# Seven quarter products instead of eight for most input slabs of the second mixer, with the weight sums on GpSimd

## The chip, the cores and the metric

One core of a Trainium2 chip runs the whole program in one launch. The metric is the device time of that launch in microseconds (us). TensorE multiplies matrices (stationary weights are loaded, then columns of the moving operand stream past them) into PSUM, which has eight banks of 128 partitions x 512 fp32. VectorE (DVE), ScalarE (ACT) and GpSimd (POOL) do the rest, and SyncE's queue (SP) issues nearly all loads from HBM. Engines wait for each other by semaphores only. All data are fp32.

## The reference

256 tokens of width 1024 pass through two blocks. The first is a gated feed-forward, a mixer (RWKV-7 time mixing beside dilated attention) and another feed-forward. The second block has two layers, each a mixer and then a dense feed-forward (layer 0) or eight experts of which two are chosen per token (layer 1). The part of the layer's mixer that the change concerns:

```python
def _mixer(h, pos, rel_table, w_in, b_gate, ...):
    z = h @ w_in                      # 1024 x 5792
    dq, dk, dv, cq, ckv, kr, gl = jnp.split(z, IN_SPLIT_IDX, axis=-1)
    ...
    o_a = _diff_attention(dq..., dk..., dv..., ...)     # 8 heads, two score maps each
    o_b = _mla(cq, ckv, kr, ...)                        # 8 heads
    g = jax.nn.sigmoid(gl + b_gate)
    g_a, g_b = g[..., :D_MODEL], g[..., D_MODEL:]
    m = g_a * (o_a @ w_branch_diff) + g_b * (o_b @ w_branch_mla)
    return m @ w_out
```

`dq` and `dk` have 1024 columns each, `gl` 2048. In the first block's time mixing the state recurrence (`wkv7_scan`) is computed in chunks of 64 tokens, with small 64 x 64 products per head.

## The kernel before, in words

**Layout.** `h_cm` holds the 256 tokens' activations, channels in the partitions: 8 tiles of 128 channels x 256 tokens. Weights come in slabs of 1024 x 512 (2 MB, 128 partitions x 4096) into a ring of four slots. A list, `stream`, fixes their order; SP goes through it and before load n waits for the last reader of load n - 4 (`last_reader`, L3168 to L3171). For a layer of the second block the order is lat, latr, dqk 0, dv 0, dqk 1, dv 1, dqk 2, uq, dqk 3, ukv, gate slabs g2 0 to 3, bmla, bdiff 0 and 1, out2 0 and 1. Slab dqk a holds the queries and keys of heads 2a and 2a + 1; the four gate slabs hold the 2048 gate columns.

**A plain slab** (`product_cm`, L312) is four output tiles of 128 columns, two to a bank, each the sum of eight matmuls of 128 x 128 weights by 128 x 256 activations. The compiler splits every fp32 matmul into two instructions, so a slab is 64 instructions in the profile. ScalarE copies the dqk banks to SBUF (L2188) and takes the gates' sigmoid straight from PSUM (L2200).

**Strassen's scheme in the feed-forwards.** Three feed-forwards already use one level of it (`pe_up_seven`, L468): the product of a slab, cut into 2 x 2 quarters, with the activations, cut into 2 x 2 quarters, is made of seven quarter products instead of eight. A unit is 7 x 8 matmuls of 128 x 128 by 128 x 128, 112 instructions. VectorE makes four sums of weight quarters (L556 to L561), and eight additions that put the seven products together (L571 to L585).

**Order of the mixer** (`pe_mixer2`, from L1978): it is written out by hand, one program per engine. On TensorE: lat, latr, dqk 0, scores 0, dv 0, dqk 1, turn 0 (transposes of the softmax weights, L2036), scores 1 (L2026), output 0 (L2047), dv 1, dqk 2, turn 1, scores 2, output 1, uq, dqk 3, turn 2, scores 3, output 2, ukv, g2 0, turn 3, MLA scores 0 (L2063), output 3, g2 1, MLA turn 0 (L2073), MLA scores 1, MLA output 0 (L2085), g2 2, the sums for the norm of the differential heads' output (L2140), MLA turn 1, the first half of g2 3, MLA output 1, the second half of g2 3, bmla, then, behind a wait for `oa_ready`, bdiff 0 and 1, and out2. Banks go round in rotation (`next_bank`), and each filling waits until the previous content of its bank was read.

**The normed output OA.** After MLA output 1 ScalarE copies it (L2215), loads a table and takes a square root (L2263); VectorE takes the reciprocal (L2394), multiplies (L2396) and scales (L2397), which sets `oa_ready`. Then `dve_merge` (L1658, L1663, L1667) multiplies the branch products by the gates.

**MLA weights.** VectorE masks the scores (L2355), takes row maxima (L2269), ScalarE the exponentials (L2172), VectorE the reciprocal of the sums and two multiplications (L2364), and TensorE turns the result (L2073).

**The recurrence** (`pe_rwkv_chunks`): eight groups of four heads by two chunks in a software pipeline. Per group and pair half, the key products (L1258) are 16 matmuls of 64 columns; the steps of the triangular solve are rounds of eight (L1237); the solved step is two such rounds with the same weights; the queries (L1317) are 16 matmuls of 64 columns.

**GpSimd** does no arithmetic on the data: it issues some loads (norm rows, L1968; the per-layer embedding tile, L1974) and clears a row.

## Time and profile before

| | us |
|---|---|
| median of 3 runs (2611.89 to 2613.22) | 2612.46 |
| the profiled execution's own time | 2612.26 |
| its span | 2610.2 |
| TensorE busy, share of the span | 97% |
| VectorE busy | 37% |
| ScalarE busy | 14% |
| GpSimd busy | 2% |

The span is divided roughly so: first feed-forward to 205 us, first mixer to 690, second feed-forward to 905, mixer of layer 0 from 908 to 1191, dense feed-forward to 1425, mixer of layer 1 from 1433 to 1717, experts to the end. A row of the profile's lists names the engine, the line of the kernel, the instruction, what it writes and reads and how often it occurs; "idle before" tells how long the engine stood still just before, and what ended that.

### The profile page before, as it was taken

The numbers are of one execution on the slowest core, as the hardware profiler recorded it, in microseconds if no ns is written. First come the engines' busy times: TensorE is split into PE (matmuls) and PEld (weight loads), VectorE is DVE, ScalarE is ACT, GpSimd is POOL, SyncE is SP. The second block draws the span as 40 slices with busy tenths as digits, with TensorE's granted clock in tenths as the row PEclk, the third lists the DMA queues.
The fourth block names the chain that finished last, engine by engine and source line by source line (L and its number), as shares of the span: only waits on it lengthen the run. The fifth ranks groups of instructions, "written<-read, shape, count | busy, mean of one in ns | idle before, by whom it ended". The sixth has DMA issues, their size and how long they took to land.

```text
span 2610.2 us, 74146 instructions
## 1 busy us (share of the span) xinstructions
PE 2539.9 (97%) x33934; PEld 2154.1 (83%) x33934; DVE 964.1 (37%) x1792; ACT 365.7 (14%) x842; POOL 42.4 (2%) x74
## 2 busy tenths in 40 slices
PE   8999999999999999999999999999999999999998
PEld 8966778887698477875994778759999998999997
DVE  5663464633477723244676233440000001000002
ACT  1001241210100023311000234120000001000000
POOL 0000000000100000000000000010000000000000
PEclk9999999999999999999999999999999999999999
DMA  6445242014344543325435434379999999999995
GB/s 259 148 144 196 105 152 103 4 36 153 142 174 153 189 169 128 133 113 193 179 108 187 165 142 166 145 246 373 427 427 426 425 426 397 427 427 427 426 425 251
DMA packets 58053, 607.72 MB, mean 233 GB/s; under 512 B 7364, under 2 KB 7492, under 8 KB 12352
## 3 DMA queue, kind: packets, MB, share of 16 engines
q1 hardware_dynamic: 52272, 587.74, 56.4%
q0 software_dynamic: 5648, 18.04, 2.2%
q8 instruction: 105, 1.72, 0.3%
q14 instruction: 28, 0.23, 0.0%
HBM read 599.66 MB, written 6.09 MB: 232 GB/s over the span
## 4 chain that ended last, share of the span: by engine, by line
PE 92%; DMA 4%; DVE 2%; issue 1%; ACT 1%; POOL 0%; SPq 0%; DVEq 0%; ACTq 0%; POOLq 0%
PE bank L312 22%; PE bank L2681 18%; PE bank L468 16%; PE bank L2694 9%; PE bank L495 7%; PE bank L322 5%; DMA slot<-in_experts 3%; PE bank L1648 3%; PE bank L1237 3%; PE bank L1634 1%; PE bank L965 1%; PE bank L1258 1%; PE bank L2613 1%; PE bank L1317 0%; PE bank L2026 0%
## 5 line engine op out<-in xcount | busy, mean ns | idle before, releaser
L2681 PE MATMUL bank<-arena,slot 128*64 128x84 f32 x14336 | 545.5, 237 | 13.7 <-issue 8.1
L2681 PEld LDWEIGHTS bank<-arena,slot 128*64 128x64 f32 x14336 | 531.8, 137 | 21.1 <-issue 16.9
L312 PE MATMUL bank<-h_cm,slot 128*128 128x256 f32 x1984 | 436.4, 381 | 0.3 <-ACT h_cm L359 0.2
L312 PEld LDWEIGHTS bank<-h_cm,slot 128*128 128x128 f32 x1984 | 376.5, 191 | 58.4 <-issue 7.9
L2880 DVE TENSOR_TENSOR ff<-ff,bank 128x168 f32<-128x168 f32 x112 | 36.9, 330 | 639.4 <-PE bank L2681 635.3
L2694 PE MATMUL bank<-ff,arena 128*64 128x84 f32 x5376 | 218.1, 237 | 2.6 <-issue 2.6
L2694 PEld LDWEIGHTS bank<-ff,arena 128*64 128x64 f32 x5376 | 205.7, 137 | 9.0 <-issue 4.4
L468 PE MATMUL bank<-arena 128*128 128x128 f32 x1584 | 187.7, 275 | 0.0
L468 PEld LDWEIGHTS bank<-arena 128*128 128x128 f32 x1584 | 182.2, 192 | 0.0
L468 PEld LDWEIGHTS bank<-h_cm,slot 128*128 128x128 f32 x1056 | 125.5, 198 | 9.9 <-issue 9.9
L468 PE MATMUL bank<-h_cm,slot 128*128 128x128 f32 x1056 | 129.4, 283 | 3.5 <-DVE h_cm L371 2.8
L312 PE MATMUL bank<-arena,slot 128*128 128x256 f32 x608 | 132.7, 379 | 0.0
L312 PEld LDWEIGHTS bank<-arena,slot 128*128 128x128 f32 x608 | 115.0, 190 | 17.0 <-issue 1.6
L2817 ACT ACTIVATE ff<-bank 128x168 f32<-128x168 f32 x112 | 34.8, 311 | 668.6 <-PE bank L2681 668.6
L322 PE MATMUL bank<-slot,h_cm 128*128 128x512 f32 (+1 forms) x288 | 119.3, 571 | 0.7 <-ACT h_cm L355 0.6
L322 PEld LDWEIGHTS bank<-slot,h_cm 128*128 128x128 f32 x288 | 53.9, 190 | 60.8 <-issue 60.0
L495 PE MATMUL bank<-arena,ff 128*128 128x512 f32 x180 | 86.5, 592 | 0.0
L1648 PE MATMUL bank<-slot,arena 128*128 128x512 f32 x192 | 82.9, 592 | 0.0
L539 ACT ACTIVATE ff<-arena 128x512 f32<-128x512 f32 x33 | 20.8, 631 | 403.3 <-DVE arena L585 403.3
L1648 PEld LDWEIGHTS bank<-slot,arena 128*128 128x128 f32 x192 | 36.3, 190 | 44.5 <-issue 44.0
L2694 PE MATMUL bank<-ff,x_tm 128*64 128x84 f32 x1792 | 69.9, 236 | 0.6 <-issue 0.6
L495 PEld LDWEIGHTS bank<-arena,ff 128*128 128x128 f32 x180 | 34.2, 190 | 43.1 <-issue 37.6
(452 smaller groups left out, 2581.0 us busy)
## 6 DMA issues: line engine op xcount, KB each, us to landing
slot<-in_experts SPq DMA_DIRECT2D x112, 2048.0 KB, 16.9
arena<-in_experts SPq DMA_DIRECT2D x84, 1024.0 KB, 12.7
slot<-in_ffn SPq DMA_DIRECT2D x22, 2048.0 KB, 8.2
x_tm<-in_experts SPq DMA_DIRECT2D x28, 1024.0 KB, 12.5
slot<-in_ffn SPq DMA_DIRECT2D x22, 1024.0 KB, 4.8
slot<-in_dense SPq DMA_DIRECT2D x11, 2048.0 KB, 7.7
slot<-in_dqk SPq DMA_DIRECT2D x8, 2048.0 KB, 8.0
slot<-in_g SPq DMA_DIRECT2D x8, 2048.0 KB, 7.7
```

The source lines that it names most:

```text
L312: ins = pe.matmul(ps[0:m, j * S:(j + 1) * S], w[:, k * width + c0:k * width + c0 + m], rhs[:, k, :], start=k == 0, stop=k == ks - 1)
L322: ins = pe.matmul(ps[:, 0:n], lhs[:, k, t * P:(t + 1) * P], w[:, k * width + c0:k * width + c0 + n], start=start and k == 0, stop=stop and ...
L468: ins = pe.matmul(ps[:, g, :], left[q][:, k, g, :], right[q][:, k, :], start=k == 0, stop=k == 3)
L495: ins = pe.matmul(PS[DOWN_BANK[q]][:, :], left[q], right[q], start=first, stop=u == U_DENSE - 1, skip_group_check=True)
L965: ins = pe.matmul(ps[:, j * S:(j + 1) * S], w[:, c0:c0 + P], h_cm[:, k, :], start=k == 0, stop=k == KD - 1)
L1237: ins = pe.matmul(ps[rows, h * width + c0:h * width + c0 + 64], left(rows, a, p, i), right(rows, a, p, i), start=True, stop=True)
L1258: ins = pe.matmul(ps[chunk_rows(c), (2 * x + i) * 64:(2 * x + i + 1) * 64], left[rows, k, tok], right[rows, k, tok], start=True, stop=True)
L1648: ins = pe.matmul(ps[:, :], src[:, k, t * P:(t + 1) * P], w[:, k * 512:(k + 1) * 512], start=k == 0, stop=k == KD - 1)
L2681: ins = pe.matmul(bank[64 * c:64 * c + 64, m * PLACES:(m + 1) * PLACES], weights[:, c0:c0 + 64], CURRENT[:, k, :], start=k == 0, stop=k == ...
L2694: ins = pe.matmul(PS[4 + d // 4][64 * c:64 * c + 64, (d % 4) * PLACES:(d % 4 + 1) * PLACES], weights[:, c0:c0 + 64], ff[:, 2 + par, kk * P ...
L2817: act.activation(ff[:, par, 0:2 * PLACES], PS[par][:, 0:2 * PLACES], ACT.Silu).then_inc(silu_ready, 1)
L2880: v.tensor_tensor(ff[:, 2 + par, 0:2 * PLACES], ff[:, par, 0:2 * PLACES], PS[2 + par][:, 0:2 * PLACES], ALU.mult).then_inc(hidden_ready, 1)
```

## The change

It has four parts.

- Slabs dqk 1, 2 and 3 and all four gate slabs of both layers go by Strassen's scheme: 112 instructions instead of 64 per slab, and four banks instead of two. Slab dqk 0 and the others stay as they are. Gate slab 3 is cut at the fourth product (1, 2, 6, 7 before MLA output 1, then 4, 5, 3).
- The four sums of weight quarters of such a slab are made by GpSimd, into a slot of the same ring: the list of loads gets an entry without a source behind each of the seven slabs, SP passes over it, and GpSimd waits for the weights and for the last reader four entries before. It also makes the four sums of activations, once per layer, in the space of the norm rows; these rows are therefore loaded only once gate slab 3 was read.
- VectorE puts the products together (eight operations of 128 x 256 per slab) at places written into its program. ScalarE no longer copies dqk 1 to 3, and takes the gates' sigmoid from SBUF, once all four banks of a slab are done. The merge waits for the sigmoids (`gates_ready`).
- In the recurrence, pairs of matmuls that have the same weights become one of twice the columns, whose moving operand lies in two places: key products, solved step, queries. The buffer XV moves for this.

```diff
+                if (name, n) in SEVEN_SLABS:
+                    stream.append(((f"sum_{name}{l}", n), None, 0))
...
-                for x, (left, right) in enumerate(((KK, DEC), (K, DEC), (KK, R), (K, R))):
+                for m, left in enumerate((KK, K)):
                     for i in range(2):
                         for c in range(2):
                             tok, k = chunk_tokens(t, c), k0 + 2 * a + i
-                            ins = pe.matmul(ps[chunk_rows(c), (2 * x + i) * 64:(2 * x + i + 1) * 64],
-                                            left[rows, k, tok], right[rows, k, tok], start=True, stop=True)
+                            at = k * S + tok.start
+                            ins = pe.matmul(out[chunk_rows(c), :, m, i, :], left[rows, k, tok],
+                                            two_places(rows, 2048 + at, 8 * 2048 + at), start=True, stop=True)
...
-                by_chunk(ps, a, P, 0, lambda rows, a, p, i: TT[a][rows, p, i, :], head_of(A_TM, g))
-                filled(by_chunk(ps, a, P, HD, lambda rows, a, p, i: TT[a][rows, p, i, :],
-                                lambda rows, a, p, i: XV[a][rows, p, i, :]), ("WU", j, a))
+                for h, (p, i) in enumerate(HEADS):
+                    for c in range(2):
+                        rows, head = chunk_rows(c), (k0 + 2 * a + i) * P + 64 * p
+                        ins = pe.matmul(ps[rows, h * P:(h + 1) * P], TT[a][rows, p, i, :],
+                                        two_places(rows, 2 * 2048 + t * D + head, XV_AT[a] + h * CHUNK), start=True, stop=True)
...
+        def pool_slab_sums(pool, l):
+            add, sums = pool.tensor_tensor, named("x_quarters")
...
+            for name, n in SEVEN_SLABS:
+                weights = first_load[f"{name}{l}", n]
+                load, w = slab_sums(l, name, n)
+                s, done, before = weights % SLOTS, slot_loaded[load % SLOTS], 16 * (load // SLOTS)
+                pool.wait_ge(slot_loaded[s], 16 * (weights // SLOTS + 1))
+                pool.wait_ge(*last_reader[load - SLOTS])
+                add(w[0], quarter_w(s, 1, 0), quarter_w(s, 1, 1), ALU.add).then_inc(done, 4)
+                pool.wait_ge(done, before + 4)
+                add(w[1], w[0], quarter_w(s, 0, 0), ALU.subtract).then_inc(done, 4)
+                pool.wait_ge(done, before + 8)
+                add(w[3], quarter_w(s, 0, 1), w[1], ALU.subtract).then_inc(done, 4)
+                pool.wait_ge(done, before + 12)
+                add(w[2], quarter_w(s, 0, 0), quarter_w(s, 1, 0), ALU.subtract).then_inc(done, 4)
...
+        def pe_slab_seven(pe, l, name, n, products):
...
+            for q in products:
+                b, c = slab_product(q)
+                key = (name, l, n, b)
+                ps = fill(pe, key, next_bank()) if c.start == 0 else PS[job[key][0]]
+                if (name, n) == SEVEN_SLABS[0] and q == 6:
+                    pe.wait_ge(named("x_quarters"), 4 * l + 4)
+                if q in (6, 7):
+                    pe.wait_ge(slot_loaded[load % SLOTS], 16 * (load // SLOTS) + (8 if q == 6 else 16))
+                out = ps[:, c].rearrange("p (g s) -> p g s", g=2)
+                for g in range(2):
+                    for k in range(4):
+                        ins = pe.matmul(out[:, g, :], left[q][:, k, g, :], right[q][:, k, :], start=k == 0, stop=k == 3)
...
+            if b == 0:
+                ch.step(v.tensor_copy(G_PART[:, 3], product(1)))
+                ins = v.tensor_tensor(out(0, 0), G_PART[:, 3], product(2), ALU.add)
+            elif b == 1:
+                ch.step(v.tensor_tensor(G_PART[:, 0], G_PART[:, 3], product(6), ALU.add))
+                ins = v.tensor_tensor(G_PART[:, 1], G_PART[:, 0], product(7), ALU.add)
+            elif b == 2:
+                drained(dve, (name, l, n, 1))
+                v.tensor_tensor(out(1, 0), G_PART[:, 1], product(4), ALU.subtract)
+                v.tensor_tensor(out(1, 1), G_PART[:, 1], product(5), ALU.add)
+                ins = v.tensor_tensor(G_PART[:, 2], G_PART[:, 0], product(5), ALU.add)
+            else:
+                drained(dve, (name, l, n, 2))
+                ins = v.tensor_tensor(out(0, 1), G_PART[:, 2], product(3), ALU.add)
+            free(ins, (name, l, n, b))
...
             mla_turn(1)
-            g2_bank(3, 0)
+            pe_slab_seven(pe, l, "g2_", 3, SEVEN[0:4])
             mla_out(1)
-            g2_bank(3, 1)
+            pe_slab_seven(pe, l, "g2_", 3, SEVEN[4:7])
...
             def g2(s):
-                for tile in range(4 * s, 4 * s + 4, 2):
-                    ps = full(act, ("g2", l, tile))
-                    for j in range(2):
-                        ins = act.activation(gates2[:, tile + j, :], ps[:, j * S:(j + 1) * S], ACT.Sigmoid,
-                                             bias=col(f"b_gate{l}", tile + j))
-                    free(ins, ("g2", l, tile))
+                for b in range(4):
+                    drained(act, ("g2_", l, s, b))
+                for tile in range(4 * s, 4 * s + 4):
+                    ins = act.activation(gates2[:, tile, :], gates2[:, tile, :], ACT.Sigmoid, bias=col(f"b_gate{l}", tile))
+                ins.then_inc(named("gates_ready"), 1)
...
             diff_weights(3)
+            gate(0, 0, 1, 2, 3)
             diff_turned(3)
-            mla_weights(0)
+            mla_weights(0, lambda: gate(1, 0, 1))
+            gate(1, 2, 3)
             mla_turned(0)
-            mla_weights(1)
+            mla_weights(1, lambda: gate(2, 0, 1))
+            gate(2, 2, 3)
...
             mla_turned(1)
-            dve.wait_ge(named("oa_rms"), l + 1)
+            gate(3, 0, 1)
+            dve.wait_ge(named("oa_stages"), 4 * l + 3)
...
-            for tile in range(0, 16, 2):
-                drained(dve, ("g2", l, tile))
+            gate(3, 2, 3)
+            dve.wait_ge(named("gates_ready"), 4 * (l + 1))
```

In `mla_weights` the two additions of the slab (`meanwhile`) stand between the row maxima and the wait for the exponentials; `SEVEN` is the order of the products, 1, 2, 6, 7, 4, 5, 3, two to a bank.

## Rows read from the trace of the kernel before

**Rows 1.** The page: busy time, granted clock, chain by engine, a gate slab's load.

```profile
PE 2539.9 (97%) x33934; PEld 2154.1 (83%) x33934; DVE 964.1 (37%) x1792; ACT 365.7 (14%) x842; POOL 42.4 (2%) x74
PEclk9999999999999999999999999999999999999999
PE 92%; DMA 4%; DVE 2%; issue 1%; ACT 1%; POOL 0%; SPq 0%; DVEq 0%; ACTq 0%; POOLq 0%
slot<-in_g SPq DMA_DIRECT2D x8, 2048.0 KB, 7.7
```

**Rows 2.** Stretches: layer 0's mixer and a plain slab (TensorE alone), a recurrence period (all engines).

```profile
908.00:1158.10 250.10, 249.38 (x1175) 1.00 0.38 143
960.57:974.38 13.81, 13.81 (x65) 1.00 0.24 97
...
475.30:488.70 13.40, 12.32 (x432) 11.53 (x432) 8.37 (x24) 3.49 (x11) 0.00 (x0) 1.00 0.02 6
```

**Rows 3.** The chain that ended last: start, us, what.

```profile
14.12 139.95 PE bank L468 x1232
...
1109.30 48.54 PE bank L312 x224
...
1223.40 137.81 PE bank L468 x1232
```

**Rows 4.** Timeline around the OA chain of layer 0.

```profile
1109.22 7.17 PE L312 MATMUL bank<-h_cm,slot 128*128 128x256 f32 x32
1113.18 12.95 DVE L2394 RECIPROCAL arena<-arena 128x2048 f32<-128x2048 f32 x1 [11.91 <-ACT arena L2263]
1126.17 2.29 DVE L2396 TENSOR_TENSOR arena<-arena 128x2048 f32<-128x2048 f32 x1
1128.50 1.29 DVE L2397 TENSOR_SCALAR arena<-arena,cols 128x2048 f32<-128x2048 f32 x1
1129.70 2.48 DVE L1658 TENSOR_TENSOR arena<-bank,arena 128x512 f32<-128x512 f32 x4
```

**Rows 5.** Groups of instructions: VectorE's sums in the second feed-forward; GpSimd's MEMSET.

```profile
L556 DVE TENSOR_TENSOR arena<-slot 128x1024 f32<-128x1024 f32 x7 | 8.5, 1219 | 0.0
L573 DVE TENSOR_TENSOR arena<-arena,bank 128x256 f32<-128x256 f32 x6 | 2.5, 420 | 0.2
...
L2960 POOL MEMSET arena<- 1x1024 f32 x1 | 0.9, 942 | 0.0
```

**Rows 6.** Timeline: dqk slab 3 with the turn behind it, gate slab 0.

```profile
1033.72 0.82 PE L2036 MATMUL bank<-consts,arena 128*128 128x128 f32 x6
1033.92 0.59 ACT L2188 COPY arena<-bank 128x512 f32<-128x512 f32 x1 [6.32 <-PE bank L312]
...
1044.42 13.98 PE L312 MATMUL bank<-h_cm,slot 128*128 128x256 f32 x64
```

**Rows 7.** Timeline around mla_weights 0 and gate slab 1.

```profile
1068.80 1.83 DVE L2364 TENSOR_TENSOR arena<-arena,ff 128x512 f32<-128x512 f32 x2
...
1076.63 1.47 PE L2073 MATMUL bank<-consts,arena 128*128 128x128 f32 x12
...
1076.84 0.84 ACT L2200 ACTIVATE arena<-bank,cols 128x256 f32<-128x256 f32 x2 [4.35 <-PE bank L312]
...
1080.66 0.65 PE L2085 MATMUL bank<-arena 128*64 128x256 f32 x4
```

**Rows 8.** Timeline of one recurrence period: rounds, queries, key products.

```profile
463.46 0.54 PEld L1237 LDWEIGHTS bank<-ff,xn 64*64 64x64 f32 x16
463.92 0.55 PEld L1237 LDWEIGHTS bank<-xn,ff 64*64 64x64 f32 x16
...
466.23 0.69 PE L1317 MATMUL bank<-arena,ff 64*64 64x64 f32 x32 [0.22 <-ACT ff L1440]
466.69 0.55 PEld L1237 LDWEIGHTS bank<-ff,xn 64*64 64x64 f32 x16
...
468.50 1.06 PEld L1258 LDWEIGHTS bank<-arena 64*64 64x64 f32 x32
...
```

More of the change, by code:

```diff
@@ L232, in two_blocks @@
         stream = []
+        SEVEN_SLABS = [("dqk_", 1), ("dqk_", 2), ("dqk_", 3)] + [("g2_", n) for n in range(4)]
         def slabs(name):
@@ L763, in two_blocks, with two_places @@
         ff_flat = ff[:, :, :].rearrange("p n s -> p (n s)")
-        X1, XV = ([ff_flat[:, (2 * a + i) * 256:(2 * a + i + 1) * 256].rearrange("p (h i s) -> p h i s", h=2, i=2)
-                   for a in range(2)] for i in range(2))
+        X1 = [ff_flat[:, 512 * a:512 * a + 256].rearrange("p (h i s) -> p h i s", h=2, i=2) for a in range(2)]
+        XV_AT = (24576, 26368)
+        XV = [arena[:, at:at + 256].rearrange("p (h i s) -> p h i s", h=2, i=2) for at in XV_AT]
+        def two_places(rows, first, second):
+            return bass.AP(arena, rows.start * 13 * 2048 + first, [[13 * 2048, CHUNK], [second - first, 2], [1, CHUNK]])
         WU = [ff_flat[:, 1024 + a * 512:1024 + (a + 1) * 512].rearrange("p (h i d) -> p h i d", h=2, i=2) for a in range(2)]
@@ L1323, in queries @@
                 drained(pe, ("WU", *g))
-                by_quadrant("QG", g, ((0, decayed, key_block(0), True, True), (1, decayed, head_of(B_TM, g), True, True)))
+                j, a = g
+                t, k0 = PAIRS[j]
+                ps = [fill(pe, ("QG", *g, c), next_bank()) for c in range(2)]
+                last = {}
+                for i in range(2):
+                    for p, c in QUADRANTS:
+                        head = (k0 + 2 * a + i) * P + 64 * p
+                        out = ps[c][64 * p:64 * p + 64, 0:256].rearrange("p (u i s) -> p u i s", u=2, i=2)
+                        last[c] = pe.matmul(out[:, :, i, :], decayed(chunk_rows(c), a, p, i),
+                                            two_places(chunk_rows(c), 4 * 2048 + t * D + head, key_block_at(a, p, i)),
+                                            start=True, stop=True)
+                for c in range(2):
+                    filled(last[c], ("QG", *g, c))
             def outputs(g):
@@ new lines, in slab_product @@
+        def slab_product(q):
+            r = SEVEN.index(q)
+            return r // 2, slice((r % 2) * S, (r % 2 + 1) * S)
+        def pe_slab_seven(pe, l, name, n, products):
+            weights = first_load[f"{name}{l}", n]
+            load, w = slab_sums(l, name, n)
+            s = weights % SLOTS
+            pe.wait_ge(slot_loaded[s], 16 * (weights // SLOTS + 1))
+            left = {1: quarter_w(s, 0, 0), 2: quarter_w(s, 0, 1), 3: w[3], 4: quarter_w(s, 1, 1), 5: w[0], 6: w[1], 7: w[2]}
+            right = {1: quarter_x(0, 0), 2: quarter_x(1, 0), 3: quarter_x(1, 1), 4: X_SUM[:, 3], 5: X_SUM[:, 0],
+                     6: X_SUM[:, 1], 7: X_SUM[:, 2]}
+            for q in products:
[10 more added lines that the diff above has]
+                        ins = pe.matmul(out[:, g, :], left[q][:, k, g, :], right[q][:, k, :], start=k == 0, stop=k == 3)
+                if c.start or q == 3:
+                    filled(ins, key)
+            if products[-1] == 3:
+                released((f"{name}{l}", n), (name, l, n, 3))
+                released((f"sum_{name}{l}", n), (name, l, n, 3))
@@ L2235, in act_mixer2 @@
             dv(1)
-            dqk(2)
             diff_out(1)
```

93 lines of the change are left out of this document (66 added, 27 removed).

## The prediction

> **What bounds the kernel now.** I read the page first: TensorE is busy for 97% of the span and is 92% of the chain that ended last, at the granted clock's upper level, 2.4 GHz, in every slice [rows 1]. Next a stretch of the second block's mixer in layer 0: 249.38 of 250.10 us are TensorE's [rows 2], and layer 1 runs the same program. So time goes there only if matmul time goes or a wait comes in; VectorE is busy for 37% of the span, GpSimd for 2% [rows 1]. Last the recurrence (the WKV chunks): a period of 13.4 us with TensorE busy for 12.3 [rows 2], small waits between. The profiled execution took 2612.26 us around a span of 2610.2; the median of the runs is 2612.46, so I sum against 2612.3.
>
> **Plain slab against Strassen slab.** A dqk or gate slab is 64 instructions of 128x256 (the compiler splits each fp32 matmul in two) and takes 13.81 us [rows 2], one of four such stretches of layer 0 with the same length. Seven quarter products are 7 x 8 x 2 = 112 instructions of 128x128. The same form runs in the dense block: 1232 in 137.81 us for 11 units, 12.53 us per unit, and 139.95 us, 12.72, in the first feed-forward [rows 3]. I take 12.65: these slabs have waits like the first one's. Saved per slab 13.81 - 12.65 = 1.16 us, between 1.09 and 1.28. That is 8% of the slab and not the 12.5% of the count of products, because a 128-column instruction costs 112 to 114 ns where half of a 256-column one costs 108 (13.81 / 64 / 2). Six of the seven slabs in each of two layers: 12 x 1.16 = **-13.9 us** (-13.1 to -15.4).
>
> **The seventh slab (gate slab 3) gives nothing.** Its halves surround the last MLA output. From its second half (1109.22) a chain runs beside TensorE: ScalarE's copy, table load and Sqrt, VectorE's reciprocal of 12.95, multiply 2.29, scale 1.29, ended at 1128.50 + 1.29 = 1129.79 [rows 4]. TensorE covers it with 32 instructions of the slab and 64 of bmla, 96 x 48.54 / 224 = 20.8 us [rows 3], to 1130.1: 0.3 us of cover to spare. Now three products, 48 x 113 ns = 5.4, and bmla's 13.9 make 19.3 against the chain's 20.6: a wait of 1.3 us before bdiff appears. Ahead of the MLA output stand four products, 64 x 113 ns = 7.2 us, instead of 6.9. Together +0.3 for the first half, and the old spare 0.3 is all that is won behind it: **0**, up to +0.5 per layer. VectorE's adds for banks 0 and 1 are done before the reciprocal can start (Sqrt ends 4 us after the MLA output begins); those for 2 and 3 come behind the scale, 4 x 0.42 = 1.7 us, then ScalarE's four sigmoids, 1.7 us (two take 0.84 [rows 7]), then the merge of bmla, 2.48 us [rows 4, 5]. TensorE needs none of it until the first bdiff bank is merged, about 7 us on, so this costs nothing, with about 1 us of cover.
>
> **VectorE's adds, 0.** Eight operations of 128x256 with PSUM input at 0.415 to 0.42 us [rows 5], 3.4 us per slab, lie under the slab's own 12.65 us. The last one ends 0.4 us behind product 3; before, ScalarE's copy of 0.59 us stood there and the scores began right behind the turn of 0.82 us [rows 6]. ScalarE loses its dqk copies. Banks: a slab now takes four of the eight in rotation. I followed the fills; the tight one is the fourth MLA score bank, which waits for the gate bank that VectorE adds behind mla_weights.
>
> **Weight sums on GpSimd.** The trace has no arithmetic on GpSimd. Below, its MEMSET of 1024 elements, one stream: 0.94 us. Above, three streams (two read, one written), 2.83 us. VectorE takes 1.22 us for the same sum [rows 5]. I take the middle, 1.9 us an operation, 7.5 a slab. What hides it: the ring. A sum's slot is free when the load four places before is read, and TensorE needs two sums after two products (+3.6 us) and all four after three (+5.4). The tightest is gate 0: slot free with dqk 3 at 1033.72, slab read from 1044.42, all four by 1049.8, so 16.1 us for four, 4.0 us each [rows 6]; gate 2 and 3 wait for their weights (a load of 7.7 us [rows 1] after the slab two before), which leaves 5.1 us each, dqk 3 about 4.8. So up to 4.0 us per operation the sums cost 0. The Trainium skill, "GPSIMD Engine Reference", Elementwise side-by-side cycle accounting, puts a two-input fp32 add at 4497 ns for 2048 elements, about 2 times VectorE, and says to use VectorE for such work; no trace here shows it, and by it the sum is the same, since its estimate of 2.3 us for 1024 also lies under 4.0. The four sums of x, half as large, run 40 us before they are read.
>
> **The ring.** Every load waits for a reader four places before, now with the sums in the count: gate 1's weights wait for the sum of dqk 3 (landing about 1042, read from 1061), bmla's for gate 2. Each has over 10 us in hand at 7.7 us a load. The norm rows now load behind gate 3, with the ple tile queued behind them on GpSimd; about 40 us pass until TensorE turns it. 0.
>
> **Stalls.** ScalarE now has four sigmoids behind the last bank instead of two, then the copies on which the attention outputs wait: VectorE's last add ends 0.6 us after the slab, the sigmoids take 1.7, two copies like the one of 0.59 [rows 6] 1.2, together 3.5 us, where TensorE arrives 4.0 us after it [rows 7], and about 3.3 us after gate slab 0; if a table load comes behind the waits, it is late by up to a microsecond, twice per layer. And VectorE must get mla_weights 0 out before gate slab 1 ends, with two adds of the slab ahead of its multiplies (slack about 2 us, from 5 [rows 7]). I book 1.0 us per layer, between 0 and 3: **+2.0** (0 to +6).
>
> **The recurrence.** The diff also joins pairs of 64-column matmuls with the same weights. Key products: 32 instructions in 1.06 us, 33 ns each, two quadrants at work. Joined, 16 of 128 columns at 113 / 2 = 56 ns: 0.90 us. The solved step: 16 in 0.46 us, twice, 0.92, to 0.90; queries 32 in 0.46, to 16 x 28 = 0.45 [rows 8]. Of the two key products per group one lies in the stretch where TensorE waits for the levels of the solve (1.1 us of the period in all [rows 2]), so its saving goes into the wait. That leaves some 0.25 us for each of 8 groups: **-2.0** (+1 if two-place operands stream worse, -3.9 if all counts). XV's move changes no work.
>
> **Sum.** 2612.3 - 13.9 + 0 + 2.0 - 2.0 = **2598.4 us**. What follows is a chain in which everything moves up, the expert loads too: they start on slots that TensorE frees. 0.2% (5.2 us) is about what a measurement of this kernel can tell from no change.
>
> **Rivals.**
> A. *VectorE held up by GpSimd.* Gate slab 2's sums start about 8 us after gate slab 0 ends and last 7.5 to 9 us; in that stretch VectorE has mla_weights' two multiplies, both inputs in SBUF, 1.83 us [rows 7]. If each waits for a running sum of 1.9 us, mla_weights is 3.8 us late against 2 us of slack, in each layer, and some short stalls elsewhere: +4 to +6, 2603. For it: these are the only two-input SBUF operations near a wait. Against: other such work has 10 us of slack. The Trainium skill, "SBUF — State Buffer", section on the two separate sides, states that VectorE with two SBUF inputs and GpSimd take a shared port pair as an exclusive lock for a whole instruction; no row of before shows it, and it is this rival's mechanism. 20%.
> B. *The sums come late: slower.* Place: TensorE's wait for the sums before products 6 and 7. It costs nothing up to 4.0 us per operation, then 4 us for each us more at gate 0, and from 4.8 and 5.1 at three more slabs. At 5.2 it eats 7 us per layer, all that the change brings. At 5.6, twice my upper bound: (6.4 + 3.2 + 2 x 2.0) x 2 = 27, less 14: 2625. Against: four times VectorE's time. 4%.
> C. *VectorE in the turn's place.* If each slab's last add comes a microsecond late for the scores or sigmoids behind it, 1.16 is given back and only the recurrence stays: 2610. Against: VectorE idles 7 us and more ahead of most slab ends. 8%.
> D. *More than forecast.* Slabs at 12.53, no stalls, all of the recurrence: 2612.3 - 15.4 - 3.9 = 2593. 12%.
> The forecast itself, 2595.5 to 2601.5: 56%.
>
> **Numbers.** The range from 2592 to 2605 holds the forecast, D and nearly all of A. Faster: forecast, A, D = 88%; same 8% (C and the edge of A); slower 4% (B).
>
> **What would show it.** Right: 112 instructions per slab in 12.5 to 12.7 us; GpSimd sums between 0.94 and 2.83 us; a wait of 1.3 us before bdiff released by VectorE's scale; mixers of about 244 us; periods of 13.2. Wrong: a TensorE wait released by GpSimd; the two multiplies of mla_weights longer than 0.92 us each; a wait before the MLA turn; a slab that takes over 13 us.

## The result, and the profile after

The changed kernel takes **2625.2 us** (2624.4 to 2625.7, 5 runs) where the kernel before took 2612.5: the ratio is 1.0049, 95% interval 1.0037 to 1.0060. It is slower by 0.5%; the prediction was 2598.4, faster, with a range up to 2605.

The page of the changed kernel: busy time, granted clock, instruction queue (packets, MB), chain by engine, the largest group.

```profile
PE 2519.3 (96%) x34094; PEld 2156.9 (82%) x34094; DVE 1041.3 (40%) x1904; ACT 359.5 (14%) x830; POOL 185.6 (7%) x138
PEclk9999999999999999999999999999999999999999
q8 instruction: 134, 2.20, 0.3%
PE 89%; DVE 5%; issue 3%; ACT 2%; DMA 1%; POOL 0%; SPq 0%; DVEq 0%; ACTq 0%; POOLq 0%
L2818 PE MATMUL bank<-arena,slot 128*64 128x84 f32 x14336 | 547.9, 237 | 33.2 <-issue 31.2
```

The same two rows of the kernel before, which had no part in the prediction.

```profile
q8 instruction: 105, 1.72, 0.3%
L2681 PE MATMUL bank<-arena,slot 128*64 128x84 f32 x14336 | 545.5, 237 | 13.7 <-issue 8.1
```

Beside [rows 1], TensorE's busy time is 20.6 us less, so the arithmetic saving arrived; all of it lies ahead of the experts, in which TensorE is busy for 829.4 us before and 829.5 us after. "Issue" is 3% of the chain where it was 1%. (DVE is at 5% where it was 2%, but that is no loss of this size: in the mixers the chain now runs through VectorE while TensorE works beside it.) The last row names the place: the experts' up-projections (L2681 before, L2818 after), the same instructions, with 31.2 us of waiting for nothing that the profile shows, where it was 8.1. The change touches no line of the experts. And TensorE's program came in 134 packets of 16 KB instead of 105.

Where the time went can be seen from the starts of the same pieces in both chains (before, after, difference in us): first block's output projection 658.59, 653.26, **-5.3**; layer 0's mixer 908.95, 903.57, -5.4; its output projection 1158.28, 1149.78, -8.5; layer 1's 1683.42, 1672.84, **-10.6**; first expert matmul 1753.94, 1742.04, **-11.9**; end +13.6. From the first expert matmul to the end of the span the kernel before takes 856.3 us and the changed one 881.8: **25.5 us** are lost in code that the change does not touch. Of the 20.6 us only 11.9 arrive at the experts; the other 8.7 are new idle time of TensorE, nearly all in three waits of each of the two mixers (2.3, 0.8 and 1.2 us, further below).

The changed kernel's stretches that answer to [rows 2]: both mixers and one recurrence period (us, then TensorE busy, its weight loads, VectorE, ScalarE, GpSimd, granted clock).

```profile
903.57:1149.78 246.21, 241.69 (x1505) 205.66 (x1506) 122.59 (x199) 68.49 (x168) 73.18 (x35) 0.99 0.39 148
1423.60:1672.84 249.24, 244.72 (x1505) 207.67 (x1506) 128.11 (x201) 70.14 (x169) 73.64 (x36) 0.98 0.40 149
486.15:499.03 12.88, 11.99 (x368) 11.37 (x369) 8.49 (x24) 3.50 (x11) 0.00 (x0) 1.00 0.02 4
```

The two mixers run the same program. Some 2.5 us of the second one's 249.24 lie at its beginning, where its first 80 matmuls take 20.5 us at a granted clock of 0.52 (1423 to 1430); in the run with the loop's head at slot 0 (below), with the same code there, they take 18.0 us at 1.00. So these 2.5 us are not the slabs' doing.

The changed kernel's chain: three Strassen slabs (dqk 1, gate 1, gate 2), then the stretch around the second expert pair's beginning.

```profile
955.35 12.51 PE bank L1799 x112
...
1054.62 14.03 PE bank L1799 x112
...
1074.86 12.70 PE bank L1799 x112
...
1946.08 8.79 issue
1954.87 3.35 PE bank L2818 x44
1958.21 1.06 issue
1959.28 3.27 PE bank L2818 x84
1962.55 1.53 PE bank L2831 x42
1964.08 1.25 issue
```

TensorE stands still for 8.79 us with no releaser, where its loop over pairs of experts goes back to its head, and again for 8.60 us at 2384.13; smaller gaps follow. Three more rows of the changed kernel: a window behind that stand and one behind a wait in layer 0's mixer (us, TensorE busy, granted clock), and the instruction queue from 1945 to 2010.

```profile
1955.00:1958.00 3.00, 3.00 (x44) 0.50 0.98 407
...
1054.00:1056.00 2.00, 2.00 (x12) 0.56 0.03 8
...
q8 instruction: 9, 0.15, 1.0%
```

Behind the stand the granted clock is 0.50, the lower of its two levels. Nine packets of program arrive where the kernel before has none. Some ten microseconds after the stand the loads of data fall to 50 GB/s for a short while: they wait for slots that TensorE frees, and SyncE's queue waits for TensorE for up to 19.2 us there. These loads run at 427 GB/s otherwise, and the lost time is not made up.

### The profile page after: what moved, and what is told of

It reads as the page before. It is cut to its first block, busy times and chain, and to the rows that moved or that the text cites. A ratio compares the mean times of both kernels' runs of the same rounds, so it can differ in the third digit from the quotient of the medians.

```text
span 2623.8 us, 74738 instructions
## 1 busy us (share of the span) xinstructions
PE 2519.3 (96%) x34094; PEld 2156.9 (82%) x34094; DVE 1041.3 (40%) x1904; ACT 359.5 (14%) x830; POOL 185.6 (7%) x138
## 4 chain that ended last, share of the span: by engine, by line
PE 89%; DVE 5%; issue 3%; ACT 2%; DMA 1%; POOL 0%; SPq 0%; DVEq 0%; ACTq 0%; POOLq 0%
PE bank L2818 20%; PE bank L471 16%; PE bank L315 13%; PE bank L2831 10%; PE bank L498 7%; PE bank L1799 5%; PE bank L325 5%; PE bank L1677 3%; PE bank L1245 2%; PE bank L1663 1%; DVE arena L2531 1%; DMA slot<-in_experts 1%; PE bank L973 1%; PE bank L2750 1%; PE bank L1268 1%
## 5 line engine op out<-in xcount | busy, mean ns | idle before, releaser
L2818 PE MATMUL bank<-arena,slot 128*64 128x84 f32 x14336 | 547.9, 237 | 33.2 <-issue 31.2
L2818 PEld LDWEIGHTS bank<-arena,slot 128*64 128x64 f32 x14336 | 533.8, 138 | 40.1 <-issue 39.7
L315 PE MATMUL bank<-h_cm,slot 128*128 128x256 f32 x1088 | 243.0, 385 | 1.3 <-ACT h_cm L358 0.6
L315 PEld LDWEIGHTS bank<-h_cm,slot 128*128 128x128 f32 x1088 | 208.9, 193 | 35.1 <-issue 6.2
L2831 PE MATMUL bank<-ff,arena 128*64 128x84 f32 x5376 | 212.1, 237 | 6.0 <-issue 5.8
L2831 PEld LDWEIGHTS bank<-ff,arena 128*64 128x64 f32 x5376 | 200.9, 137 | 11.9 <-issue 10.0
L471 PEld LDWEIGHTS bank<-h_cm,slot 128*128 128x128 f32 x1056 | 123.4, 196 | 8.9 <-issue 8.9
L471 PE MATMUL bank<-h_cm,slot 128*128 128x128 f32 x1056 | 127.1, 280 | 2.8 <-DVE h_cm L374 2.8
L1799 PE MATMUL bank<-xn,slot 128*128 128x128 f32 x896 | 102.9, 275 | 0.0
L1799 PEld LDWEIGHTS bank<-xn,slot 128*128 128x128 f32 x896 | 101.3, 192 | 0.3 <-issue 0.3
L1799 PEld LDWEIGHTS bank<-h_cm,slot 128*128 128x128 f32 x672 | 80.4, 197 | 2.5 <-issue 2.3
L1799 PE MATMUL bank<-h_cm,slot 128*128 128x128 f32 x672 | 82.1, 280 | 0.0
```

The lines of the kernel that those rows point to most:

```text
L315: ins = pe.matmul(ps[0:m, j * S:(j + 1) * S], w[:, k * width + c0:k * width + c0 + m], rhs[:, k, :], start=k == 0, stop=k == ks - 1)
L471: ins = pe.matmul(ps[:, g, :], left[q][:, k, g, :], right[q][:, k, :], start=k == 0, stop=k == 3)
L1799: ins = pe.matmul(out[:, g, :], left[q][:, k, g, :], right[q][:, k, :], start=k == 0, stop=k == 3)
L2818: ins = pe.matmul(bank[64 * c:64 * c + 64, m * PLACES:(m + 1) * PLACES], weights[:, c0:c0 + 64], CURRENT[:, k, :], start=k == 0, stop=k == ...
L2831: ins = pe.matmul(PS[4 + d // 4][64 * c:64 * c + 64, (d % 4) * PLACES:(d % 4 + 1) * PLACES], weights[:, c0:c0 + 64], ff[:, 2 + par, kk * P ...
```

## The theories

CODE: TensorE's program is fetched in packets of 16 KB, which are 256 instructions of 64 bytes. The loop over pairs of experts is 1685 instructions, under 7 x 256 = 1792. By the compiled program its head stands at slot 32 of a block before and at slot 104 after (1024 instructions less by the joined pairs, 1352 more by the slabs, together 72 slots), both plus instructions of the loader that the file does not show. By this theory the changed loop reaches into an eighth block, and what it needs at its head is no longer there when it goes back. By the file alone it would not reach it (104 + 1685 = 1789), so the theory needs some instructions of the loader. The Trainium skill, "Runtime: NRT & Kernel Launch", section Instruction fetch mechanics, says that TensorE's instruction memory holds 2048 instructions, is filled sequentially in blocks of 256, and that a branch out of the present window stalls. DATA, the rival: the experts' loads begin at another time, or meet a ring standing two slots further on. It would make the place of the code irrelevant.

For the mixers, LOCK: the prediction's rival A (operations of VectorE stand still while a sum of GpSimd runs), at other instructions than it named.

## Experiments on the place of the code

There were two edits of one line. The first puts the loop's head at a chosen slot, with filler ahead of it; the second names the loop's closing branch at the head of each turn, so that its target is fetched ahead of time.

```
-                with pe.Fori(0, N_EXPERTS // 2) as pair:
+                with nc.Fori(0, N_EXPERTS // 2, engines=[pe.engine], head_slot={pe.engine: 0}) as pair:
or
+                with nc.Fori(0, N_EXPERTS // 2, engines=[pe.engine], hint_back_edge=True) as pair:
```

**The changed kernel, head at slot 0.** 

> The changed kernel, with nothing else altered than the place of TensorE's expert loop in its program: filler ahead of the loop's head puts the head at the start of a block of 256 instructions (16 KB, the size of one packet of the instruction queue), so that the loop of about 1685 instructions lies in 7 blocks. Theory CODE (the 25.5 us lost in the experts are instruction fetches: by the compiled program the changed loop reaches from slot 104 of one block, plus a few instructions of the loader, into an eighth block, where the loop before began at slot 32 and stayed in seven): the two stands of 8.79 and 8.60 us go, and with them the gaps of 1 to 2.4 us behind them; the experts take 856 us again and the time is 2599 to 2602 us. Theory DATA (the experts' loads meet a ring that stands two slots further on, or start at a worse time): the place of the code changes nothing, 2625 us, both stands still there.

Measured: 2598.8 us, ratio to before 0.9950 (0.9934 to 0.9965), 107 instruction packets. The 26 us are back, and the two stands are gone (longest wait for "issue" at L2818 1.4 us, 7.2 in all). DATA falls: the ring and the loads' order are the changed kernel's, and the loss is gone.

**The kernel before, head at slot 160.** 

> The kernel before, with the head of TensorE's expert loop moved to slot 160 of a block of 256 instructions by filler, so that the loop of about 1685 instructions lies in eight blocks; no computation and no transfer of data is changed. Theory CODE: two stands of about 9 us before the second expert pair of each layer's back edge, gaps behind them, 2632 to 2640 us. Theory DATA: no change, 2612 us.

Measured: 2634.8 us, ratio 1.0092 (1.0071 to 1.0112), 133 packets. TensorE's waits in its experts (us in total, times, longest):

```profile
PE bank L2681 <- issue: 32.9, 33, 8.7
```

That is the whole loss, in a kernel with none of the change's computation.

**How far it may reach: slots 100, 111, 128.** The same edit with other numbers.

> The kernel before, the head of TensorE's expert loop at slot 100 of a block of 256 instructions. 100 + 1685 = 1785 lies under 7 x 256 = 1792: the loop still lies in seven blocks. Theory SEVEN BLOCKS (the stands come when the loop touches an eighth block): no change, 2611 us, no stand over 3 us in the experts. A theory of mere shift (the further from slot 32, the more is fetched anew) gives part of the 24 us that slot 160 cost: 2616 to 2630.

> The same with the head at slot 111, eleven instructions further: 111 + 1685 = 1796 is four instructions past the end of the seventh block. Theory SEVEN BLOCKS: the whole price, 2632 to 2637 us, with two stands of about 9 us and about 28 more packets in the instruction queue. Theory of mere shift: as at slot 100, within 2 us.

> The kernel before, TensorE's expert loop with its head at slot 128 of a block of 256 instructions; nothing else. At slot 111 (four instructions of the loop in an eighth block) it cost nothing, at slot 160 (53 instructions in it) 24 us. Theory EIGHTH BLOCK (the price comes whole once the loop has more than a handful of instructions in the eighth block; here 128 + 1685 = 1813, 21 of them): 2632 to 2637 us, 27 or so more instruction packets. Theory of a proportional price (the further the tail reaches, the longer the stand): between, about 2620.

Measured: slot 100 ratio 1.0004 (0.9994 to 1.0013), 105 packets; slot 111 ratio 1.0001 (0.9991 to 1.0011), 105 packets; slot 128 ratio 1.0103 (1.0073 to 1.0133), 2638.5 us, 132 packets. The price comes whole between 111 and 128. The expectation for slot 111 failed: the bound of seven blocks is not exact, since four instructions should lie in the eighth there, and that cost nothing. The mere shift costs nothing at all.

Slot 111 also puts a question to the explanation of the changed kernel, whose head stands at slot 104 by the file, less than 111. The loader's instructions must make up the difference. The packets behind the loop say so. The code there is the same in all kernels, so their number depends on the head's slot alone. The instruction queue from 2550 us on, with the head at 128, with the head at 160, and in the changed kernel:

```profile
q8 instruction: 1, 0.02, 0.1%
q8 instruction: 2, 0.03, 0.2%
q8 instruction: 2, 0.03, 0.1%
```

It is one packet with the head at 0, 100, 111 or 128 and two with it at 160, and two in the changed kernel and in every variant of it whose head was left where it falls. So its head stands beyond 128, if the number goes with the slot as these runs show. How many instructions the loader puts ahead is not on record.

**The branch named.** 

> The changed kernel, its code where it was, with one instruction added at the head of each turn of TensorE's expert loop that names the loop's closing branch, so that its target is fetched ahead of time. Theory HEAD ALONE (the stand of 8.8 us is the fetch of the first block behind a taken branch): the stands of 8.79 and 8.60 us go, the gaps of 1 to 2.4 us behind them stay: 2606 to 2612 us. Theory ALL BLOCKS (with a loop of eight blocks each block is fetched anew in every turn, and the first branch is only the first of them): the stands shrink by a part, 2615 to 2622 us.

> The kernel before with the expert loop's head at slot 160, which cost 24 us, and with the loop's closing branch named at the head of each turn. Theory NAMED TARGET (the loop fits into what TensorE holds even with its tail in an eighth block; what evicts the first block is a fetch beyond the loop's end, and with the target named that fetch goes to the first block): 2610 to 2613 us, 105 to 107 instruction packets. Theory POSITION (the name does nothing and the one instruction had moved the loop): 2632 to 2637 us, about 133 packets.

Measured: the changed kernel with the branch named 2596.7 us, ratio 0.9946 (0.9929 to 0.9963), 107 packets; the kernel before at slot 160 with the branch named 2611.3 us, ratio 1.0001 (0.9992 to 1.0011). Its instruction queue and its longest wait for "issue":

```profile
q8 instruction: 106, 1.74, 0.3%
PE bank L2681 <- issue: 8.8, 24, 1.5
```

Both expectations of the first run were too pessimistic. At a slot where the loop certainly touches an eighth block nothing is fetched anew once the target is named, so the loop fits into what TensorE holds. The counts go further: up to 1940 us every variant of the kernel before has 104 packets, with the head at 100 or 111 as at 160, so the eighth block is there in all of them. What comes next in the changed kernel are two packets together, between 1949.5 and 1950.2, in the stand. That one of them is a fetch beyond the loop's end which has driven out the first block, and that this fetch starts only some instructions into the eighth block (hence slot 111), agrees with all seven runs, but a trace does not say which block a packet holds: this part is argued. The Trainium skill, "Advanced Engine Details and Errata", section ISA Cache, says "Only 2 cache lines!" beside the 128 KB of TensorE; the 105 packets of the kernel before, which runs its seven-block loop four times, speak against two lines for TensorE: by the compiled program it has 27,096 instructions, 105.8 blocks, so each block came once. The changed one has 27,424, 107.1 blocks, and fetched 134: nine again on each of the loop's three ways back (1945 to 2010, 2160 to 2215, 2380 to 2430).

## Experiments on the two parts of the change

**The joined pairs alone** (the recurrence's part of the diff on the kernel before) and **the slabs alone** (the rest of it). 

> The kernel before with the change's other part alone: pairs of 64-column matmuls of the recurrence joined into 128-column ones, every mixer slab plain as before. It removes 1024 TensorE instructions, 4 blocks of 256 exactly, so the expert loop stands in its block as before. By the prediction's term it saves 2.0 us (+1 to -3.9): 2610.4. By the changed kernel's chain, in which the first mixer ends 5.3 us earlier, it saves 5 to 6: 2606.5 to 2607.5. Both CODE and DATA expect experts of 856 us.

> The kernel before with the Strassen slabs and GpSimd's weight sums alone, the recurrence with its 64-column pairs. TensorE's expert loop stands at the same slot as in the changed kernel (1352 instructions are added). Theory CODE: the experts lose the 25.5 us as in the changed kernel: 2625.2 + 5.3 = 2630.5 us. Theory DATA expects the same if the ring's place is the cause, and with a load timing as cause somewhere between 2606 and 2630, as the mixer ends 5 us later relative to nothing that loads. The two layers' mixers of the second block are as in the changed kernel: about 246 and 249 us.

> The Strassen slabs alone, the recurrence as before, the expert loop's head at slot 0. If the two parts and the loop's place add up: 2598.8 + 5.9 = 2604.7 us by the joined pairs' own saving (2611.05 - 2605.19 = 5.9), so that the slabs alone are worth 6 us and not the 11.9 of the prediction. If the joined pairs save less beside the slabs (a wait takes it up), 2601 to 2603.

Measured: joined pairs 2605.2 us, ratio 0.9974 (0.9964 to 0.9983); slabs with the code where it falls 2630.2, ratio 1.0068 (1.0047 to 1.0088), 138 packets; slabs with the head at slot 0 2607.2, ratio 0.9982 (0.9973 to 0.9992). So the joined pairs are worth 5.9 us (2611.1 - 2605.2; 4 to 9 by the interval), three times the term of the prediction, the slabs 4.7 (2611.9 - 2607.2; 2 to 7 by the interval) and not 11.9, and the place of the code costs 23. The two gains multiply to 0.9956, inside the interval of the changed kernel at slot 0.

## Experiments on the mixers

The changed kernel's VectorE and GpSimd around gate slab 0 of layer 0 (start, us, engine, line).

```profile
1034.91 5.20 DVE L2454 TENSOR_SCALAR arena<-arena,ff 128x128 f32<-128x128 f32 x4
1040.15 5.61 DVE L2459 SCALAR_TENSOR_TENSOR arena<-arena,ff 128x128 f32<-128x128 f32 x4
1045.92 0.42 DVE L1824 COPY ff<-bank 128x256 f32<-128x256 f32 x1 [0.16 <-DVE arena L2459]
...
1035.04 2.37 POOL L1767 TENSOR_TENSOR slot<-slot 128x1024 f32<-128x1024 f32 x1 [0.69 <-PE bank L325]
1037.56 2.41 POOL L1769 TENSOR_TENSOR slot<-slot 128x1024 f32<-128x1024 f32 x1
1040.11 2.36 POOL L1771 TENSOR_TENSOR slot<-slot 128x1024 f32<-128x1024 f32 x1
1042.61 2.48 POOL L1773 TENSOR_TENSOR slot<-slot 128x1024 f32<-128x1024 f32 x1
```

The kernel before at the same two operations:

```profile
1043.12 1.01 DVE L2333 TENSOR_SCALAR arena<-arena,ff 128x128 f32<-128x128 f32 x4
1044.16 1.41 DVE L2338 SCALAR_TENSOR_TENSOR arena<-arena,ff 128x128 f32<-128x128 f32 x4
```

Eight small operations of VectorE take 10.8 us instead of 2.4 while four sums of GpSimd run. Gate slab 0's adds (L1824 on) queue behind them and end at 1049.3; on ScalarE a load of the sigmoid's table and four sigmoids follow, then the copy that TensorE waits for. ScalarE there, and TensorE's waits in layer 0's mixer of the changed kernel:

```profile
1049.40 1.28 ACT L2325 ACT_TABLE_LOAD   x1 [11.80 <-DVE arena L1836]
1050.69 1.70 ACT L2325 ACTIVATE arena<-arena,cols 128x256 f32<-128x256 f32 x4
...
PE bank L2172 <- ACT arena L2330: 2.3, 1, 2.3
PE bank L315 <- DVE arena L2534: 1.2, 1, 1.2
PE bank L2210 <- ACT arena L2337: 0.8, 1, 0.8
```

**GpSimd's sums moved.** The changed kernel with the head at slot 0, and:

```
                 pool.wait_ge(*last_reader[load - SLOTS])
+                if (name, n) == ("g2_", 1):
+                    pool.wait_ge(named("diff_weights"), 4 * l + 4)
```

> The changed kernel with the loop's head at slot 0, and GpSimd waiting with gate slab 1's weight sums until VectorE has the fourth set of differential weights out; those sums are then made about 8 us before TensorE needs them. Theory LOCK (VectorE's operations that read and write SBUF alone stand still while GpSimd's sums run; that makes diff_weights(3) 8 us late, and gate slab 0's adds and sigmoids with it): the four scalings take 1.01 us again where they took 5.20, the four multiply-adds 1.41 where they took 5.60, and TensorE's wait of 2.25 us before differential output 3 falls to 0.3 to 1.0 us; layer 1 likewise: 2 to 4 us less than 2598.8, 2595 to 2597. Theory QUEUE (the multiplies are long by themselves, or for reasons of their buffers): 5.20 and 5.60 us as before, 2598.8.

Measured: 2598.3 us, ratio 0.9953 (0.9937 to 0.9970), no gain over slot 0 alone. The trace says why. VectorE at the same two operations and at mla_weights' multiplies, then TensorE's waits:

```profile
1034.18 1.01 DVE L2456 TENSOR_SCALAR arena<-arena,ff 128x128 f32<-128x128 f32 x4
1035.23 1.40 DVE L2461 SCALAR_TENSOR_TENSOR arena<-arena,ff 128x128 f32<-128x128 f32 x4
1060.51 4.96 DVE L2488 TENSOR_TENSOR arena<-arena,ff 128x512 f32<-128x512 f32 x2
...
PE bank L2212 <- ACT arena L2339: 1.8, 1, 1.8
PE bank L2174 <- ACT arena L2332: 0.8, 1, 0.8
PE bank L2200 <- DVEq L2490: 0.8, 1, 0.8
```

The eight operations are short again and the wait before output 3 falls from 2.3 to 0.8, as LOCK said. What was won was lost again further on: mla_weights' two multiplies, 1.83 us before [rows 7], now meet gate slab 2's sums and take 4.96. That is rival A at the very instructions it named. The expected 2 to 4 us were a miss, because only the one lock was priced.

**Tables early, with the sums moved and without.** In the slab's sigmoids and ahead of the last MLA output's copies, a small operation that brings the table in before the wait:

```
             def g2(s):
+                act.activation(stat[:, 32 + 4 * l + s:33 + 4 * l + s], ident[:, 0:1], ACT.Sigmoid)
...
             g2(2)
+            act.activation(stat[:, 40 + l:41 + l], ident[:, 0:1], ACT.Sqrt)
             mla_out(1)
```

With the sums moved, run twice:

> As the last, and ScalarE runs a small Sigmoid before it waits for each gate slab's adds, and a small Sqrt ahead of the copies of the last MLA output, so that the table loads of 1.28 us come before the waits and not behind them. Theory TABLE (each load of 1.28 us stands on TensorE's path before differential output 3, before MLA output 0 and before the differential output projection): the waits of 0.78 us before MLA output 0 and 1.2 us before that projection go, and what is left before output 3: 2 to 2.7 us per layer, 2590 to 2593 us. Rival: the loads only move, and a later one (Exp of the next softmax) becomes late in their place: no better than the last kernel.

> The fastest version once more, head at slot 0, beside its two relatives on this chip: 2585 us, ratio to the kernel before 0.990. If the 13.5 us against the version without the early tables were partly luck of that chip, 2588 to 2591.

With the named branch in place of the slot, and without the moved sums:

> The fastest version with the named closing branch in place of the fixed slot. Theory NAMED TARGET: the same time within 3 us, 2583 to 2588. Theory POSITION gives no sure number: this code's slot differs by no TensorE instruction from the kernel in which the name worked, so the same 2585.

> The changed kernel, loop head at slot 0, with the early Sigmoid and Sqrt, but GpSimd's sums for gate slab 1 where the change has them. Theory BOTH (diff_weights(3) is 8 us late under GpSimd's sums and carries gate slab 0's adds to 1 us before the sigmoids; the early tables take 1.28 us off each of the three waits per layer, 2.25, 0.78 and 1.2 us): 3.3 us per layer less than 2598.8, 2592 us, and 5 to 7 us behind the version with both. Theory TABLES ALONE: as the version with both, 2585 us.

Measured, ratios to before: 0.9904 (0.9888 to 0.9921), 2584.8 us; the same kernel again 0.9920 (0.9904 to 0.9937), 2590.8; named branch 0.9908 (0.9892 to 0.9925), 2587.5; tables without the moved sums 0.9935 (0.9919 to 0.9952), 2592.0. By the totals the tables are worth 8.6 to 13 us with the sums moved, so a part of the first run's 13 was its luck, as the expectation of the second had allowed; without them they are worth 4 us, inside the intervals. The expectation named BOTH, 2592, was met. The two mixers of the traces (us, layers 0 and 1) say more:

| head at slot 0, and | layer 0 | layer 1 |
|---|---|---|
| nothing else | 246.2 | 246.7 |
| sums moved | 245.2 | 246.9 |
| tables early | 242.6 | 245.7 |
| both | 240.4 | 242.6 |
| both, second run | 242.5 | 242.6 |
| both, branch named in place of the slot | 241.0 | 244.6 |

In the first run of both, the two edits are worth 5.8 and 4.1 us, more than each alone added up (1.0 and 3.6 in layer 0, nothing and 1.0 in layer 1): each alone leaves a wait that the other takes away. Runs of the same edits differ by 2 us in a mixer, so smaller differences between rows say nothing. The difference is one wait: in the second run of both TensorE waits 1.9 us for VectorE's multiplies in layer 0, with the branch named it does so in layer 1, and in the first run in neither. There two engines arrive at about the same time.

**The kernel before with the same early tables.** 

> The kernel before with ScalarE's small Sigmoid and Sqrt ahead of its waits in the second block's mixers, as in the fastest kernel so far, and nothing else. Theory STALLS OF THE CHANGE (the early tables gained 13 us there because the Strassen slabs' adds on VectorE put the sigmoids behind the slab's end, which the plain slabs don't do): TensorE waits for nothing in these mixers before, so 2610 to 2611 us, no change. Rival: the table loads were in the way of both kernels: 5 us less or more.

Measured: ratio 1.0003 (0.9994 to 1.0013). The table loads were hidden before; the change uncovered them.

**Gate slab 2's sums moved too.**

```
+                if (name, n) == ("g2_", 2):
+                    pool.wait_ge(named("mla_weights"), 2 * l + 1)
```

> The fastest version (head at slot 0, early tables, gate slab 1's sums behind diff_weights(3)) with gate slab 2's sums behind the two multiplies of mla_weights 0 as well; by the last trace that leaves about 13 us for four sums of 2.4. Theory LOCK (the prediction's rival A): the two multiplies take 1.83 us again where they took 3.98, and no wait of TensorE for VectorE is left in either mixer, 240 to 241 us for layer 0's and 242 to 243 for layer 1's: 2583 to 2587 us. Rival LATE SUMS (the prediction's rival B in small: the sums now start too late): TensorE waits for GpSimd before products 6 and 7 of gate slab 2, 2 us or more per layer: 2590 us or more.

Measured: **2584.3 us, ratio 0.9897 (0.9880 to 0.9913)**, the lowest of all, though its interval overlaps those of the versions with both edits; the traces are what sets it apart. Its multiplies, and all that TensorE waits for in layer 0's mixer:

```profile
1059.19 1.83 DVE L2492 TENSOR_TENSOR arena<-arena,ff 128x512 f32<-128x512 f32 x2
...
PE bank L2155 <- issue: 0.3, 1, 0.3
PE bank L315 <- ACT h_cm L362: 0.2, 1, 0.2
```

1.83 us again, no wait left for VectorE or ScalarE's gates. The mixers take 239.8 and 240.8 us, from 249.3 and 250.3.

## Why the prediction was wrong

**The step that failed is the sentence that follows its sum**: that behind the changed stages everything moves up, the expert loads too. Everything did move up, by 11.9 us, and then 25.5 were lost in TensorE's own instruction fetch. The prediction counted instructions for their time and never for their place: neither the sum nor a rival had the program's length in it. Rival B's 2625 us is the measured time, but by a mechanism that did not happen: no wait of TensorE for GpSimd's sums appears.

With the loop's place put right the kernel takes 2598.8 us, the forecast within 0.4. That is luck: against the forecast the slabs gave 1.8 us more and the recurrence 3.9 more, and the stalls cost 7 more. The terms one by one:

- **Slabs, forecast -13.9.** Undisturbed slabs take 12.50 and 12.70 us against 13.81 and 14.01 for plain ones in the same places, 1.31 saved each and not 1.16: 12 x 1.31 = -15.7. The 12.65 was too high for the dqk slabs, and the plain gate slab 2 took 14.01, not 13.81. One slab met the prediction's own sign of being wrong, over 13 us: gate slab 1, 14.03 in layer 0 of the changed kernel, behind a wait and at the lower clock; that is booked under the stalls.
- **Gate slab 3, forecast 0 with a wait of 1.3 us before bdiff.** The wait is 1.2 us, released by VectorE's scale (L2534, the operation of [rows 4]). From gate slab 3's start to the output projection: 57.35 us before (1100.93 to 1158.28), 57.47 in the changed kernel at slot 0 (1090.41 to 1147.88). Right.
- **Stalls, forecast +2.0 (0 to +6).** This term was mis-sized; it measured about 9. Per layer: 2.3 us before output 3, 0.8 before MLA output 0, and some 1.6 that no term held: after the standstill the granted clock is at its lower level for about three microseconds. The instructions of output 3 take 2.9 us at slot 0 (1051.04 to 1053.97, granted clock 0.50) where they took 1.3 before (1061.67 to 1062.98). The prediction did name the table load behind the waits and gave it up to a microsecond; it did not see that VectorE itself would be 8 us late.
- **Rival A** had the right mechanism, and its price was near (+4 to +6; the slabs fell 7 short), but the prediction looked for it at the two multiplies with both inputs in SBUF. The operations hit first were diff_weights' scalings (one tensor read, 1.01 to 5.20 us) and its multiply-adds (two, 1.41 to 5.61), which the prediction had passed over with "other such work has 10 us of slack". The Trainium skill, "SBUF — State Buffer", section "SBUF: two separate sides", has the lock also for VectorE operations with one input in a two-port mode, which the prediction left out; the trace agrees with it in the scalings' 5.20 us, though it does not name their mode.
- **GpSimd's sums, 1.9 us taken, under 4.0 free.** They take 2.35 to 2.67 us, inside the bounds, and TensorE never waited for them. The estimate of 2.3 us that the prediction worked out from the Trainium skill, "GPSIMD Engine Reference", Elementwise side-by-side cycle accounting, was nearer than its own 1.9.
- **Recurrence, forecast -2.0 (+1 to -3.9).** It gave -5.9 alone. The joined products take what was forecast (the solved step 0.90 us, L1310 x16). What failed is that half of the key products' saving would vanish in the wait for the solve. Over five periods (475.21 to 542.11 before, 473.19 to 537.67 after) TensorE's busy time fell by 0.37 us a period (61.85 to 60.02 us), as the prediction's own prices give with both key products counted (2 x 0.16 + 0.02 + 0.01 = 0.35). Its idle time did not take this up but fell as well, from 1.01 to 0.89 us a period. So the mean period went from 13.38 to 12.90, 3.9 us over eight; the other 1.4 to 2 lie at the first and last groups. That 3.9 is also the prediction's figure "if all counts" is chance: its prices give 0.35 a period, 2.8 us, and 0.19 with one key product, not the 0.25 that it took.

So at slot 0: -15.7 + 9 - 5.9 = -12.6 against -12.3 measured. The first two, -6.7, are what the two mixers of that run show (246.2 and 246.7 us, from 249.3 and 250.3); the slabs alone measured -4.7, with 6.7 inside the interval.

## What to carry to other kernels

When a change adds or removes instructions on an engine that later runs a long loop, ask where that loop's blocks of code will lie, and name the loop's closing branch or fix its head: it cost nothing here and protects 24 us. Look at the instruction queue's packet count before looking at arithmetic, beside the program's length in blocks: here 105 to 105.8 and 107 to 107.1 went with no loss, 134 to 107.1 with 25 us. When work is given to GpSimd, list every VectorE operation that reads and writes SBUF in the same stretch, not only those with two inputs, and let GpSimd wait for those that have someone waiting behind them.

## What the runs showed of the hardware

- TensorE runs a loop of 1685 instructions four times without fetching it again (105 packets in all at slots 100 and 111). With its tail further in an eighth block, each of the three ways back fetches nine packets (132 to 138 in all), with TensorE standing still for 8.6 to 8.8 us at the first and the last; at the second, behind 14 us of other matmuls, the longest stand is 2.3 to 2.9 us.
- Beside running GpSimd sums of 2.4 us, a 128x128 scaling on VectorE took 1.3 us and not 0.25 (5.20 and 1.01 for four). The sums beside it stretched little: 2.36 to 2.48 us, where 2.35 is the shortest in the trace.
- A wait of 2.3 us brought the granted clock to 0.56 in the next microseconds of matmuls (1054 to 1056); behind one of 1.0 us (tables early, alone) it stayed at 1.00. With 1.6 us of slower matmuls behind 2.3 us of waiting, the wait cost 1.7 times its length. It is no rule of length: behind the stand of 2.41 us at 2178.79 the granted clock stayed at 1.00.
